# Two-block transformer kernel on one Trainium2 core: a new order of VectorE's work in the mixer's attention loop

## The reference, cut to what matters

```python
p = h @ w_in[l]
attn = mla_group(...)                   # 8 heads, two query tiles of 128 rows
u = a * sigmoid(g)                      # the convolution's input, 512 channels
y = conv(u, conv_w, 31 taps) + conv_b
conv = silu(layer_norm(y))
x = x + concatenate([attn, conv]) @ w_out[l]
```

## Time and profile before

| | |
|---|---|
| median of 3 runs | 2329.58 us (2329.37 to 2334.75) |
| profiled execution | 2332.28 us |
| its span, first to last instruction | 2330.6 us |
| mean granted TensorE clock | 0.99 |
| busy: PE, DVE, ACT | 2262.6, 1604.6, 1104.1 us |
| the two mixers' heads and tails | about 276 to 342 and 807 to 871 us |

### The profile page before, as it was taken

How to read it: one execution, slowest core, us unless ns; L and a number is a source line. 1 busy time by engine, 2 the same in 40 slices (tenths; PEclk the granted TensorE clock), 3 DMA queues, 4 the chain that set the end, 5 groups by cost and what they waited for, 6 DMA issues and landing times.

```text
span 2330.6 us, 37335 instructions
## 1 busy us (share of the span) xinstructions
PE 2262.6 (97%) x13816; PEld 1967.7 (84%) x13816; DVE 1604.6 (69%) x2710; ACT 1104.1 (47%) x1752; POOL 112.7 (5%) x155
## 2 busy tenths in 40 slices
PE   9999989999999989999999999999999999999998
PEld 8998769998998779997777778888888888888888
DVE  6667867667667867776554555444546989988896
ACT  5443344435443345445555543333434666565664
POOL 0000000000000000212121201001100000000000
PEclk9999999999999989999999999999999999999999
DMA  8655226655564226565334431221221222222222
GB/s 325 229 201 180 73 91 241 231 209 199 206 228 170 91 82 225 201 232 98 68 72 79 69 102 64 73 73 64 73 82 63 91 90 81 81 81 90 81 99 91
DMA packets 83068, 301.88 MB, mean 130 GB/s; under 512 B 10404, under 2 KB 10788, under 8 KB 82468
## 3 DMA queue, kind: packets, MB, share of 16 engines
q1 hardware_dynamic: 78336, 284.72, 35.1%
q0 software_dynamic: 2048, 4.20, 3.2%
q10 hardware_dynamic: 2600, 11.81, 1.4%
HBM read 299.64 MB, written 1.05 MB: 129 GB/s over the span
## 4 chain that ended last, share of the span: by engine, by line
PE 74%; DVE 19%; ACT 4%; issue 3%; DMA 0%; DVEq 0%; ACTq 0%; another core or an unknown queue 0%
PE ps L751 48%; PE ps L799 11%; DVE wsplit L2200 3%; PE ps L863 3%; DVE work L2947 2%; PE ps L1388 2%; DVE work L2959 2%; PE ps L1249 1%; DVE work L2422 1%; PE ps L1112 1%; PE ps L1126 1%; PE ps L1102 1%; DVE work L2979 1%; ACT wsplit L1516 1%; DVE work L2991 1%
## 5 line engine op out<-in xcount | busy, mean ns | idle before, releaser
L751 PE MATMUL ps<-hsplit,wsplit 128*128 128x256 f32 (+1 forms) x8376 | 1379.7, 322 | 27.6 <-DVE wsplit L2200 12.0
L751 PEld LDWEIGHTS ps<-hsplit,wsplit 128*128 128x128 f32 x8376 | 1204.7, 191 | 160.4 <-DVE wsplit L2200 19.0
L2200 DVE TENSOR_TENSOR wsplit<-ring,wsplit 128x1024 fp32r<-128x1024 f32 x465 | 574.4, 1237 | 346.5 <-ACT wsplit L1516 344.8
L1516 ACT ACTIVATE wsplit<-ring 128x1024 fp32r<-128x1024 f32 x463 | 488.4, 1057 | 515.2 <-PE ps L751 391.6
L799 PE MATMUL ps<-wsplit,fsplit 128*128 128x512 f32 x1056 | 256.5, 392 | 1.9 <-DVE fsplit L2334 1.7
L799 PEld LDWEIGHTS ps<-wsplit,fsplit 128*128 128x128 f32 x1056 | 192.6, 188 | 40.0 <-issue 3.3
L2296 DVE SCALAR_TENSOR_TENSOR work<-ring,work 128x1024 f32<-128x1024 f32 x96 | 120.4, 1254 | 1.6 <-DMA ring<-panels 1.6
L1596 ACT ACTIVATE work<-ps 128x256 f32<-128x256 f32 x88 | 33.8, 384 | 161.0 <-PE ps L751 161.0
L2422 DVE SCALAR_TENSOR_TENSOR work<-work,vec 128x256 f32<-128x256 f32 x240 | 106.6, 481 | 3.5
L751 PEld LDWEIGHTS ps<-wsplit,hsplit 128*128 128x128 f32 x768 | 95.5, 197 | 4.5 <-issue 3.0
L751 PE MATMUL ps<-wsplit,hsplit 128*128 128x256 f32 x768 | 97.1, 289 | 1.1 <-DVE wsplit L2200 1.1
(11 more groups left out here) (367 smaller groups left out, 2295.7 us busy)
## 6 DMA issues: line engine op xcount, KB each, us to landing
ring<-panels SPq DMA_DIRECT2D x539, 512.0 KB, 4.1
work<-latent_weights ACTq DMA_DIRECT2D x2, 2304.0 KB, 11.8
work<-rpb POOLq DMA_DIRECT2D x64, 64.0 KB, 6.6
work<-conditions ACTq DMA_DIRECT2D x6, 512.0 KB, 5.0
cst<-constants ACTq DMA_DIRECT2D x1, 1408.0 KB
work<-x SPq DMA_DIRECT2D x2, 512.0 KB, 5.0
work<-post_rows ACTq DMA_DIRECT2D x2, 512.0 KB, 4.0
cT<-ctx ACTq DMA_DIRECT2D x1, 1024.0 KB, 6.7
```

Source lines behind the costliest of these rows:

```text
L751: ins = mm(out_, w(a), x(b), start=start and n == 0, stop=stop and n == 2, **kw)
L1516: af(wsplit[:, split_slot(name, n), 0, :], ring[:, slot, :], ACT.Copy).then_inc(high_ready, 1)
L2200: tt(parts[:, 1, :], ring[:, slot, :], parts[:, 0, :].bitcast(fp32), ALU.subtract)\
```

## The change

Five edits, the same in both layers. Ahead of the loop, VectorE does 4 taps of the last group and not 10, and low half 1 moves into head 1; three more taps stand behind the first two maxima. In the loop, three taps stand behind heads 0, 2, 3, 4 and 5 (before: 0, 2, 3, 4); behind the fourth head's product, two taps follow the low part and not four, and no low half; low halves 2 and 3 move to the ends of heads 4 and 6, and low half 4 behind the loop. TensorE's clock-keeping matmuls ahead of heads 1 and 2 become 2 each. ScalarE and VectorE split panel 5 between the two pairs of convolution outputs.

```diff
@@ TensorE, mixer @@
                     if h < 3:
-                        keep_clock(2, 12 if h == 0 else 4)
+                        keep_clock(2, 12 if h == 0 else 2)
@@ ScalarE, mixer, in the loop over the two pairs p @@
                     af(hsplit[:, 0, 4 + 2 * p:6 + 2 * p, :], mix[:, 4 + 2 * p:6 + 2 * p, :], ACT.Copy).then_inc(mix_high, 1)
+                    if p == 0:
+                        high("wout", l, 5)
                 nc.scalar.preload_act_table_set("natural_log_exp_and_others")
-                for n in range(5, 8):
+                for n in range(6, 8):
                     high("wout", l, n)
@@ VectorE, mixer @@
                 gated(3)
-                low("wout", l, 1)
-                taps(3, 10)
+                taps(3, 4)
...
                 maxima(0)
                 maxima(1)
+                taps(3, 3)
...
                     if h == 2:
                         out_low(0)
+                    if h in (0, 2, 3, 4, 5):
+                        taps(3, 3)
                     if h == 1:
-                        low("wout", l, 2)
-                    elif h < 5:
-                        taps(3, 3)
+                        low("wout", l, 1)
...
                     if h in (3, 5):
                         taps(3, 2)
                         out_low(h // 2)
-                        taps(3, 4)
-                        if h == 5:
+                        if h == 3:
+                            taps(3, 2)
+                        else:
                             taps(3, CONV_K)
-                        low("wout", l, h // 2 + 2)
+                    if h in (4, 6):
+                        low("wout", l, h // 2)
+                low("wout", l, 4)
                 out_low(3)
...
                         .then_inc(mix_split_ready, 1)
-                for n in range(5, 8):
+                    if p == 0:
+                        low("wout", l, 5)
+                for n in range(6, 8):
                     low("wout", l, n)
```

## The result

The changed kernel takes **2316.86 us** as the median of 6 runs (2316.08 to 2319.04), the kernel before 2329.47 (2327.29 to 2334.75, also 6): the ratio is 0.9943 with a 95% interval from 0.9929 to 0.9956, 13.3 us (10.3 to 16.5). The forecast was 2314.7, 14.9 us less than before. The profiled execution took 2316.08 us, its span 2314.4, 16.2 less than before's.

A forecast was written before the change was run, and what follows sets the result against it. TensorE, busy 97%, bounds the kernel; its mixer idles come from VectorE's queue and cost clock. First layer 6.4 + 1.6 = 8.0 us, second 6.9, together 14.9 off 2329.58: median 2314.7, range 2308.5 to 2321.5.

The forecast's parts named there:

- The walk of the queues: First layer's mixer: engine queues stepped through with profiled durations, giving each step's time; 6.4 us gained by the variance.
- low halves 2 and 3 would give some of the gain back: Heads 4 and 6: low half 2 makes a 1.9 us TensorE idle before copy 5; low half 3 some 0.9 late.
- The fillers' cut: Ahead of heads 1 and 2, 4 to 2 matmuls: fits within the gain, as VectorE ends later than TensorE.
- The sixth panel's split: End of the mixer: TensorE's 1.49 us wait on low half 5 goes, 1.6 us gained in the first layer.
- The clock terms of the sum: Mixers: 0.8 us lost in output panel 1, variance left at half clock, 1.06 less gain in the second layer.
- The fall in panel 1: Output panel 1, after the new idle before copy 5: clock comes down, costing 1.5 us at most, taken as 0.8.
- The sum of squares I left at the half clock: Variance after head 7: kept at 3.63 us for eight matmuls, where the sum over channels took 1.89.
- the treatment of the clock as a property of the mixer: Second layer's mixer: 1.06 us less had been lost to the clock, so gain 6.9 us against 8.0 in the first.
- Rival C: Early heads: clock falls too, where TensorE waits about 1 us for copy 3; 2.5 us a layer, 2319.7; chance 0.18.
- Rival B: Mixers: new idle before copy 5 costs no clock, variance runs like the sum; 2.6 us a layer, 2309.5; chance 0.20.
- D: Ring: low halves 1, 2 and 3 cost their full 1.14 us each; gain 3 to 4 us, 2326; chance 0.08.
- E: Head 0 to variance: too few fillers leave the clock at 1.2 GHz; +4.1 us a layer, 2337.8; chance 0.04.

The follow-up runs named there:

- the undisturbed mixer: First mixer of the unedited kernel before, profiled again: no stretch at granted clock 0.50, 56.6 us from first score to last output panel's closing matmul; run's ratio 0.9994.
- the second profile: The changed kernel run and profiled again with no edit: median 2318.02 us, ratio 0.9942 to the kernel before, mixers 55.2 and 55.3 us.
- the padded kernels: Clock-keeping matmuls added in long TensorE waits: changed kernel (8 each ahead of values 5, 7) 2314.95 us; kernel before (20 opening fillers, 8 ahead of values 4) 2325.22.

## Why the prediction was right, and where it was not

**The walk of the queues** held to about 0.4 us at every point, first layer. The mixer of after starts 0.19 us later than before's; with that taken off, the first four rows agree to 0.05 us and the last four come 0.3 to 0.4 earlier than forecast.

| step | forecast | after |
|---|---|---|
| first maxima | 279.3 | 279.53 |
| transposes 0, behind the fillers | 282.5 | 282.66 |
| copy 4 | 296.4 | 296.62 |
| copy 5, with the new idle of TensorE | 300.2, idle 1.9 | 300.38, idle 1.89 |
| sum over channels | 306.9 | 306.73 |
| centring | 308.8 | 308.66 |
| values 7, behind low half 3 | 311.75 | 311.54 |
| sum of squares | 312.45 | 312.25 |

That the fillers and not the maxima would bound the opening, that low halves 2 and 3 would give some of the gain back ahead of copies 5 and 7, and that the clock would fall in panel 1 were all in the first layer's trace. The last two low halves moved behind the loop brought 4.6 us back, so what was given back was real. The fillers' cut was costed at nothing, and the run with none showed nothing.

**The sixth panel's split** was put at 1.6 us a layer and gave 1.75 in the first. The panel's second pair, 1.0 us later on ScalarE, delayed nothing.

**The clock terms of the sum** were single figures for what turned out to be draws. The fall in panel 1 was put at 0.8 us. Against the undisturbed mixer, whose sum over the channels starts 27.64 us behind the first score, it cost 0.4 in the first layer of after and nothing in the second, and 0.6 and 0.8 in the second profile. That is why the last four rows of the table are early. The sum of squares I left at the half clock of the earlier trace rows on the ground that the heads ahead of it were as thin. Panel 2 began 3.12 us behind it in before, 2.42 in the first layer of after and 1.60 in the second (3.03 in before's second), so that the first profile gained 0.7 and 1.4 us more than forecast; in the second profile it was 3.17 and 2.85, about as forecast.

**The step that failed** is the treatment of the clock as a property of the mixer. I took 1.06 us off the second layer, because before had lost less there, and counted 6.9 for it; in the profiles it gained 9.3, as much as the first. The comparison rested on two draws: the same first mixer of before takes 63.4 or 56.6 us. Of the 18.5 us between the profiled mixers some 7.5 are order and 11 the clock in these two executions; of the 13.3 between the timed runs some 7.5 are order and about 6 the clock. Rival C named this possibility in its last sentence (timed runs that lose less than the profiled one) at the price of its own mechanism, 2319.7; it should have had one for itself, since the runs of before were already 5 us apart, and the measured 2316.86 lies between the two.

**Why the total came out so near** in spite of it is in part luck. Of the forecast's 14.9 some 7.5 are order, so that it counted 7.4 for the clock; this came from one profile, and the timed runs happened to lose nearly as much, about 6. The profiles themselves are farther off: the profiled mixers gained 3.6 us more than the 14.9, and the part behind them, which the change does not touch, lost 2.1. That is the clock as well. Before, then after, the same 24 matmuls of the second block behind the same wait:

```profile
2272.53 3.13 PE L751 MATMUL ps<-hsplit,wsplit 128*128 128x256 f32 x24 [2.68 <-DVE wsplit L2200]
```

```profile
2255.85 5.49 PE L751 MATMUL ps<-hsplit,wsplit 128*128 128x256 f32 x24 [2.67 <-DVE wsplit L2202]
```

In the second profile of the changed kernel they took 3.14, so this fall is not the change's. Such falls come and go: over all profiles this part took 1459.4 to 1464.3 us, in the same instructions, and twice for the same kernel 1459.4 and 1462.6 (before), 1461.5 and 1460.9 (after). The medians, over more such draws, came to 12.6 us less in the first comparison and 13.5 in the second (2331.49 and 2318.02), on either side of the ratio's 13.3.

**Rival B** (the clock holds) is what the second mixer of after did in the first profile; **C** had no part through heads 0 to 4, whose clock stayed full in every profile of the changed kernel; **D** and **E** did not happen. The Trainium skill's account of the clock lost in the waits between bursts (TensorE: Matmul & The Clock Gate, "HAM oscillation") fits the padded kernels, where filling the waits kept the clock at 1.00 in every head, though the page tells it of waits of some 3 to 5 us and here 1.90 us was enough in one execution and not in another; its use against the thinner fillers doesn't fit, since TensorE only waited 0.5 us longer there.

**What stays open** is what decides, in one execution, whether a given wait of 1.9 us costs the clock. I tried nothing that would tell.

## What to carry to other kernels

Write out the queue of the engine that is late in a ring of short steps, and move what nobody waits for out of it, into a stretch in which that engine waits anyway; durations from the timeline then give each step to a few tenths. Where TensorE waits a microsecond or two at a time, split the gain into order and clock before you believe it, by profiling the same kernel twice or by padding the waits: the order is there in every run, the clock only in some, and parts tried alone need not add up. To compare one stage in two profiles, line it up by its instructions and not by its time in the span.

## What the runs showed of the hardware

One program's wait of 1.90 us, at the same place, was followed by a granted clock of 0.50 in one execution (from 284.8 us on) and of 1.00 in the next, and cost 1.9 us in the head behind it or nothing. The same held of a wait of 2.67 to 2.68 us in the second block: the 24 matmuls behind it took 5.49 us in one profile of the changed kernel and 3.14 in the other. Waits of 0.75 to 0.94 us were followed by a full clock in all heads of the changed kernel and its variants, but two of 0.88 and 0.65 around nothing but short matmuls were followed by the half clock in the padded kernel before, in both layers, and by the full clock in the first mixer of before's second profile. Eight matmuls whose result nobody reads, put into each wait of 1.9 us, made the changed kernel 2 to 3 us faster by the medians (2314.95 against 2316.86 and 2318.02).
